# Bank adds ahead of VectorE's other work, row sums moved between the halves, and value chunks asked before the last unit

## The chip, the cores and the metric

The kernel runs on one core of a Trainium2 chip. The metric is the device time of one launch in microseconds (us). It has five engines with an instruction stream each: TensorE (PE, with its weight loads shown as PEld), VectorE (DVE), ScalarE (ACT), GpSimd (POOL) and SyncE (SP, which issues transfers). They are ordered only by semaphores that the program waits on.

## The reference

One layer of an encoder over 1024 tokens of width 1024 in float32: an RMS norm, a combined projection, a pooling mixer beside dilated window attention, an output projection, and then the expert layer (PEER), on which the change acts. Each token has 8 retrieval heads, each picks 16 of 16384 experts, and

```
ue = u[expert]
ve = v[expert]
act = gelu(einsum('thkd,td->thk', ue, ht))
return einsum('thk,thkd->td', gate * act, ve)
```

The layer's output is added to the residual stream and normed once more.

## The kernel before

The kernel has several stages; the first 1798 us (mixer, queries and their top 16, the products with all of `u`) are not touched. The change is in the last one, the products with `v`.

The 8 token tiles of 128 are treated in three ways. **Five tiles** (DT = 5) are computed densely: for each of 128 chunks of 128 experts, a matrix of weights (activation `a_raw` times gate `g_raw`, both reloaded from DRAM) is multiplied with the value chunk `v_raw`. **One tile** (PT = 1) gathers its value rows 4 x 128 at a time (`v_row`) and sums them by small matmuls into the two banks `wide`, 32 steps in all (`step`). **Two tiles** (VT = 2) gather their rows (`d_row`, a ring of 6) and VectorE adds each to `yg` with a weight (`add_row`, L1467): 256 row sums.

The dense part. Float32 accuracy comes from splitting: ScalarE rounds to `v_hi` and `a_hi`, VectorE computes the remainders `v_lo` (`lower_v`, L1474) and `a_lo` (`lower_a`, L1428), and TensorE does three products (L1881). The 128 chunks go in 16 groups of 8 (GT = 8). A group has two halves: first the 8 chunks with three tiles, then the same 8 chunks with two tiles, 32 halves in all. Every tile has two PSUM banks of 512 columns, so a half of three tiles fills banks 0 to 5 and one of two tiles banks 0 to 3. A product of three tiles is 18 matmuls of 128 x 128 by 512, one of two tiles is 12. At a half's end VectorE adds its banks to `y` in SBUF (`add_half`, L1440, two adds a tile); the first product of the next half waits, tile by tile, for the adds of the same banks (`y_done`).

VectorE's order is written out as a loop over n = 0 ... 255, one step per product. In step n it multiplies the weights of step n + 1 (`gated`, L1420), computes `a_lo` of step n, then if due the remainder of one value chunk of the next group (in the steps 13, 14, 15, 0, 1, 2, 3, 4 of each 16), a selection matrix (`pick`), row sums by `rows_added`, and, in steps 2 and 10 of 16, the adds of the half that has just ended. `rows_added(n)` spreads the 256 row sums evenly over the steps 3 to 238. `a_hi` and `a_lo` have 4 slots (RA = 4), so `a_hi` of step n waits for the product of step n - 4.

GpSimd issues the gathers: in its step n the rows of VectorE's step n + 2, moved on by the ring's 6, each after the row whose slot it takes was added; and after every `step` of TensorE four gathers of `v_row`.

SyncE's queue is in program order. The weights come in units of 4 chunks (`load_unit`: `a_raw` and `g_raw`, 0.75 MB each for three tiles, 0.5 MB each for two), four units a group; a unit waits until VectorE has multiplied all of the unit whose place it takes. The 8 value chunks of the next group (0.5 MB each, a ring of 6) are asked as 4 behind a group's second unit, 2 behind the third, 2 behind the fourth. The last two wait for the remainders of the next group's first two chunks.

At the start of the stage SyncE asks the five tiles of `y`, the two of `yg`, the value chunks 6 and 7, and then goes on with units.

Of the kernel before, what the change touches and what calls it, by code (L numbers as in the profile page):

```python
# [11 lines left out]
P = 128  # L12
# [24 lines left out]
DT = NT - NGT  # L37
DS = DT * P
MH = DS // 2
TT = (3, DT - 3)  # L40
# [23 lines left out]
GT = 8  # L64
NG = NK // GT
HALVES = 2 * NG
VJ = 4
# [2 lines left out]
PT = 1  # L70
VT = NGT - PT
DR = 6
STEPS = PT * P // 4
TILE_STEPS = P // 4
GROUP_STEPS = STEPS // NG
VR = 6
# [21 lines left out]
def steps_after(h, j):  # L98

    return [h] if j == {0: 6, HALVES - 1: 2}.get(h, 4) else []  # L100


def rows_added(n):

    return min(max((n - 3) * VT * P // (HALVES * GT - 20), 0), VT * P)


QT = S // 4
# [40 lines left out]
def build(nc, x, g_mix, w_in, w_pool, pool_scale, w_out, g_ffn, w_q, subkeys, u, u_rows, v, g_final,  # L149
          ident_c, iota_c, bias01_c, bias2_c, sel_c, edge_c, inv_c, out):  # L150
    ctx = ExitStack()
    with ctx:
        base = (nc.sbuf_base + 63) // 64 * 64

        def at(name, kb, shape, dt=F32):

            return nc.alloc_sbuf_tensor_at(name, shape, dt, offset=base + int(kb * 1024))

        def sem(name):
            return ctx.enter_context(nc.semaphore(name))  # L160
# [91 lines left out]
        y = [at(f"y{i}", base, [P, D]) for i, base in enumerate((64, 75, 112, 116, 120))]  # L252
# [20 lines left out]
        x1_d = nc.dram_tensor("x1_d", [NT, P, D], F32).ap()  # L273
# [74 lines left out]
        v_in = [sem(f"v_in{k}") for k in range(VR)]  # L348
        d_in = [sem(f"d_in{k}") for k in range(DR)]
        yd_in = sem("yd_in")  # L350
# [3 lines left out]
        y_in = sem("y_in")  # L354
# [58 lines left out]
        def half_width(h):  # L413

            return TT[h % 2] * P

        def tiles_done(h):

            return DT * (h // 2) + TT[0] * (h % 2)
# [16 lines left out]
        def _(sp):  # L436
# [83 lines left out]
            def load_v(j):  # L520

                if j >= VR:
                    sp.wait_ge(vl_done, j - VR + 1)
                sp.dma_start(v_raw[:, j % VR, :], v[j, :, :]).then_inc(v_in[j % VR], 16)

            def load_a(n):

                j, w, s = GT * (n // 4) + VJ * (n % 2), half_width(n // 2), n % 2
                t0 = n // 2 % 2 * WA
                sp.dma_start(a_raw[s][:, :, 0:w], act_d[j:j + VJ, :, t0:t0 + w]  # L530
                             .rearrange("j p t -> p j t")).then_inc(a_in[s], 16)

            def load_g(n):

                j, w, s = GT * (n // 4) + VJ * (n % 2), half_width(n // 2), n % 2
                t0 = n // 2 % 2 * WA
                sp.dma_start(g_raw[s][:, 0:w // TW, :], g_d[t0 // TW:(t0 + w) // TW, :, j:j + VJ, :]
                             .rearrange("b p j t -> p b (j t)")).then_inc(g_in[s], 16)

            def load_unit(n):  # L540

                sp.wait_ge(pd_done, VJ * (n - 1))
                load_a(n)
                load_g(n)
# [26 lines left out]
                sp.wait_ge(act_out[s], 16 * stores_before(ITEMS + s))  # L571
            sp.wait_ge(m1_done, 2 * ITEMS)
            sp.wait_ge(uh_gate, 1)
            for i in range(DT):
                sp.dma_start(y[i][:, :], x1_d[i]).then_inc(y_in, 16)
            sp.wait_ge(row_used, ROWS)
            for k in range(PT, NGT):
                sp.dma_start(yg[k][:, :], x1_d[DT + k]).then_inc(yd_in, 16)

            for j in range(VR, GT):  # L580
                load_v(j)
            for g in range(NG):
                more = range(GT * (g + 1), GT * (g + 2)) if g + 1 < NG else ()
                load_unit(4 * g + 2)
                load_unit(4 * g + 3)
                for j in more[:VJ]:
                    load_v(j)
                if more:
                    load_unit(4 * g + 4)
                for j in more[VJ:VR]:  # L590
                    load_v(j)
                if more:
                    load_unit(4 * g + 5)
                for j in more[VR:]:
                    load_v(j)
            sp.wait_ge(vl_done, NK)
            sp.dma_start(yg[0][:, :], x1_d[DT]).then_inc(ya_in, 16)
            sp.dma_start(gain2[:, :], bcast_row(g_final)).then_inc(gain_in, 16)
# [8 lines left out]
        def _(pool):  # L607
# [60 lines left out]
            def gather_v(k):  # L668

                n, s = k // 4, k % 4  # L670
                if n:
                    pool.wait_ge(step_done, n)
                else:
                    pool.wait_ge(ut_ev, 1)
                nc.gpsimd.indirect_dma_start(v_row[s][:, :], None, v_rows,  # L675
                                             bass.IndirectOffsetOnAxis(ids_t[:, 0, TW * s + n:TW * s + n + 1], 0)
                                             ).then_inc(row_in[s], 16)

            def gather_d(k):

                if k >= DR:
                    pool.wait_ge(yd_done, k - DR + 1)
                c = (PT + k % VT) * P + k // VT
                nc.gpsimd.indirect_dma_start(d_row[k % DR][:, :], None, v_rows,  # L684
                                             bass.IndirectOffsetOnAxis(ids[:, c:c + 1], 0)).then_inc(d_in[k % DR], 16)

            pool.wait_ge(row_used, ROWS)
            for k in range(2):
                pool.wait_ge(g_out[k], 16 * PAIRS)
            for k in range(DR):  # L690
                gather_d(k)
            for k in range(4):
                gather_v(k)
            for n in range(HALVES * GT):
                for k in range(*(min(rows_added(n + d) + DR, VT * P) for d in (2, 3))):
                    gather_d(k)
                for m in steps_after(n // GT, n % GT):
                    for s in range(4):
                        if m + 1 < STEPS:
                            gather_v(4 * (m + 1) + s)  # L700
# [326 lines left out]
        def _(dve):  # L1027
# [77 lines left out]
            for c in range(2):  # L1105
                for hf in range(2):
                    n = 2 * c + hf
# [54 lines left out]
            for n in range(GROUPS * UNITS + 2):  # L1162
# [6 lines left out]
                m = n - (GROUPS - 1) * UNITS - 6  # L1169
# [56 lines left out]
            for n, i in enumerate(ORDER):  # L1226
                dve.wait_ge(x_in[i], 32)
                for hf in range(2):
                    m = 2 * n + hf
# [194 lines left out]
            def lower_a(n):  # L1424

                dve.wait_ge(ah_done, n + 1)
                w = half_width(n // GT)
                V.tensor_tensor(a_lo[:, n % RA, 0:w], prod[:, n % 2, 0:w], a_hi[:, n % RA, 0:w],  # L1428
                                ALU.subtract).then_inc(al_done, 1)

            def add_half(h, q):

                n = tiles_done(h) + q
                dve.wait_ge(tile_done, n + 1)
                t = TT[0] * (h % 2) + q
                for c in range(2):
                    cols = slice(c * HALF, (c + 1) * HALF)
                    if h >= 2:
                        dve.wait_ge(y_done, 2 * (n - DT) + c + 1)
                    V.tensor_tensor(y[t][:, cols], y[t][:, cols], bank[2 * q + c][:, :], ALU.add).then_inc(y_done, 1)  # L1440
# [29 lines left out]
            def lower_v(g, j):  # L1470

                n = GT * g + j
                dve.wait_ge(vh_done, n + 1)
                V.tensor_tensor(v_lo[:, j, :], v_raw[:, n % VR, :], v_hi[:, j, :], ALU.subtract).then_inc(vl_done, 1)  # L1474

            gated(0)
            for n in range(HALVES * GT):
                if n + 1 < HALVES * GT:
                    gated(n + 1)
                if n < GT:  # L1480
                    lower_v(0, n)
                lower_a(n)
                done = n - RA - 1
                if done >= 0 and done // GT % 2 and done // GT + 1 < HALVES:
                    lower_v(done // GT // 2 + 1, done % GT)
                if n == 0:
                    dve.wait_ge(uh_act, 1)
                    V.tensor_tensor(uh[:, :].rearrange("p (t k) -> p t k", t=NGT),
                                    uh[:, :].rearrange("p (t k) -> p t k", t=NGT), gate_g[:, :, :],
                                    ALU.mult).then_inc(uh_gate, 1)  # L1490
                if n == 1:
                    dve.wait_ge(ut_done, 1)
                    V.tensor_copy(ids_t[:, :, :], wide[:, 0:PT * P].rearrange("p (t k) -> p t k", t=PT))
                    V.tensor_copy(gate_t[:, :, :], wide[:, HALF:HALF + PT * P]
                                  .rearrange("p (t k) -> p t k", t=PT)).then_inc(ut_ev, 1)
                    dve.wait_ge(ut_ev, 1)
                    for k in range(2):
                        pick(k)
                done = n - RA - 1
                if done >= 0:  # L1500
                    for k in steps_after(done // GT, done % GT):
                        if k % TILE_STEPS == TILE_STEPS - 1 and k + 1 < STEPS:
                            add_rows(k // TILE_STEPS)
                        if k + 2 < STEPS:
                            pick(k + 2)
                for k in range(rows_added(n), rows_added(n + 1)):
                    if k == 0:
                        dve.wait_ge(uh_gate, 1)
                        dve.wait_ge(yd_in, 16 * VT)
                    add_row(k)  # L1510
                h = n // GT
                if n % GT == 2 and h:
                    if h == 1:
                        dve.wait_ge(y_in, 16 * DT)
                    for q in range(TT[(h - 1) % 2]):
                        add_half(h - 1, q)
            add_rows(PT - 1)
            dve.wait_ge(gain_in, 48)
            for n, i in enumerate(FINAL):
# [503 lines left out]
```

## Time and profile before

| | us |
|---|---|
| median of 3 runs | 2845.58 (2843.27 to 2847.0) |
| profiled execution | 2851.25 |
| its span | 2849.5 |
| PE busy | 2694.0 (95%) |
| DVE busy | 2065.5 (72%) |
| POOL busy | 1415.5 (50%) |
| ACT busy | 904.6 (32%) |

The span is the time from the first to the last recorded instruction. The product stage starts near 1798 us. In the views a "waited for" line gives the total of the waits in us and their number; an idle time in square brackets stands behind the instruction that ended it, with what released it.

### The profile page before, as it was taken

What the parts mean: (1) busy time and instruction counts of PE and PEld (TensorE: products, weight loads), DVE (VectorE), ACT (ScalarE), POOL (GpSimd) and SP (SyncE); (2) the same over time, 40 slices, a digit from 0 to 9 for tenths busy, and PEclk for the clock granted to TensorE, in tenths of its full rate; (3) what the DMA queues carried; (4) which work ended last, traced back from release to release, by engine and by line L of the source; (5) the groups of instructions that cost most, each with busy time, mean ns of one, the idle gap of its engine ahead of it and who ended that gap; (6) DMA issues with size and microseconds to landing.
All of it is one profiled execution on the core that took longest, in us unless ns stands there. A gap on an engine that the chain in (4) does not pass through costs nothing.

```text
span 2849.5 us, 43062 instructions
## 1 busy us (share of the span) xinstructions
PE 2694.0 (95%) x15691; PEld 2359.4 (83%) x15691; DVE 2065.5 (72%) x4758; ACT 904.6 (32%) x1750; POOL 1415.5 (50%) x960
## 2 busy tenths in 40 slices
PE   7999979998999999999999999979999998999998
PEld 6776658998999999999999999757767776777776
DVE  6022263699888989999999953668787777778774
ACT  4222341322222222356666622312222222222222
POOL 1111030446566677765565565535565554656640
PEclk9999989999999999999999999989999999999999
DMA  3101031436777888899999999989999999999993
GB/s 140 45 30 30 23 121 51 126 116 224 247 273 258 285 280 275 281 334 381 382 377 377 384 342 332 340 308 358 349 369 359 330 365 326 352 368 358 354 331 135
DMA packets 301905, 763.34 MB, mean 268 GB/s; under 512 B 22992, under 2 KB 138064, under 8 KB 298960
## 3 DMA queue, kind: packets, MB, share of 16 engines
q0 software_dynamic: 110592, 402.70, 38.4%
q1 hardware_dynamic: 191184, 359.13, 36.6%
q8 instruction: 55, 0.90, 0.1%
q14 instruction: 74, 0.61, 0.1%
HBM read 669.47 MB, written 92.27 MB: 267 GB/s over the span
## 4 chain that ended last, share of the span: by engine, by line
PE 54%; DVE 19%; issue 7%; DMA 4%; POOL 2%; ACT 1%; another core or an unknown queue 0%; SPq 0%; DVEq 0%; ACTq 0%
PE bank L1537 22%; PE bank L1881 20%; PE bank L1845 5%; DVE u_row L1332 4%; DMA g_raw<-g_d 3%; PE bank L1773 2%; PE bank L1756 2%; DVE yg L1467 2%; DVE y L1440 1%; PE wide L1901 1%; POOL w_lo L622 1%; DVE prod L1420 1%; DVE rest_k L1259 1%; DVE ix L1262 1%; DVE eq L1319 1%
## 5 line engine op out<-in xcount | busy, mean ns | idle before, releaser
L1537 PE MATMUL bank<-h_hi,w_hi 128*128 128x320 f32 (+1 forms) x2400 | 574.4, 321 | 16.4 <-POOL w_lo L622 12.8
L1537 PE MATMUL bank<-h_hi,w_lo 128*128 128x320 f32 (+1 forms) x2400 | 557.5, 314 | 0.0
L1537 PE MATMUL bank<-h_lo,w_hi 128*128 128x320 f32 (+1 forms) x2400 | 557.1, 313 | 0.0
L622 POOL TENSOR_TENSOR w_lo<-w_raw,w_hi 128x1024 fp32r<-128x1024 f32 x144 | 368.2, 2557 | 336.1 <-ACT w_hi L910 280.7
L1332 DVE CUSTOM_DVE_ANT_0 u_row<-wide,u_row 128x1024 f32<-128x1024 f32 x384 | 450.3, 1221 | 80.1 <-DMA u_row<-in_u_rows,ids 73.2
L684 POOL DMA_INDIRECT d_row<-in_v,ids x256 | 368.2, 1438 | 277.3 <-DVE yg L1467 231.6
L1881 PE MATMUL bank<-v_hi,a_hi 128*128 128x512 f32 x1272 | 408.1, 403 | 73.2 <-DVE y L1440 59.9
L631 POOL DMA_INDIRECT u_row<-in_u_rows,ids x384 | 391.3, 1019 | 111.5 <-issue 76.8
L1537 PEld LDWEIGHTS bank<-h_hi,w_hi 128*128 128x128 f32 x2400 | 401.1, 190 | 22.9 <-POOL w_lo L622 14.6
L1537 PEld LDWEIGHTS bank<-h_lo,w_hi 128*128 128x128 f32 x2400 | 406.7, 189 | 3.9
L1537 PEld LDWEIGHTS bank<-h_hi,w_lo 128*128 128x128 f32 x2400 | 405.5, 189 | 3.9
L1881 PE MATMUL bank<-v_lo,a_hi 128*128 128x512 f32 x1272 | 401.1, 397 | 0.0
L1881 PE MATMUL bank<-v_hi,a_lo 128*128 128x512 f32 x1272 | 400.0, 396 | 0.0
L1881 PEld LDWEIGHTS bank<-v_hi,a_hi 128*128 128x128 f32 x1272 | 239.2, 192 | 158.6 <-DVE y L1440 69.0
L990 ACT ACTIVATE a_hi<-prod 128x384 fp32r<-128x384 f32 (+1 forms) x256 | 120.6, 471 | 741.1 <-PE bank L1881 605.8
L1467 DVE SCALAR_TENSOR_TENSOR yg<-d_row,uh,yg 128x1024 f32<-128x1024 f32 x256 | 326.3, 1281 | 6.4 <-issue 3.4
L1881 PEld LDWEIGHTS bank<-v_lo,a_hi 128*128 128x128 f32 x1272 | 244.1, 192 | 53.4
L1881 PEld LDWEIGHTS bank<-v_hi,a_lo 128*128 128x128 f32 x1272 | 244.3, 192 | 52.9
L611 POOL TENSOR_TENSOR w_lo<-w_raw,w_hi 128x1024 fp32r<-128x1024 f32 x36 | 87.0, 2418 | 404.8 <-ACT w_hi L707 404.8
L1428 DVE TENSOR_TENSOR a_lo<-prod,a_hi 128x384 fp32r<-128x384 f32 (+1 forms) x256 | 125.2, 489 | 222.9 <-ACT a_hi L990 185.6
L675 POOL DMA_INDIRECT v_row<-in_v,ids_t x128 | 181.2, 1416 | 194.2 <-PE wide L1901 133.4
L904 ACT ACTIVATE act_st<-bank 128x320 f32<-128x320 f32 x200 | 76.3, 432 | 338.7 <-PE bank L1537 238.4
(213 smaller groups left out, 3682.5 us busy)
## 6 DMA issues: line engine op xcount, KB each, us to landing
w_raw<-in_u SPq DMA_DIRECT2D x128, 512.0 KB
v_raw<-in_v SPq DMA_DIRECT2D x128, 512.0 KB
act_d<-act_st SPq DMA_DIRECT2D x128, 320.0 KB
g_d<-g_st SPq DMA_DIRECT2D x20, 2048.0 KB
a_raw<-act_d SPq DMA_DIRECT2D x32, 768.0 KB
g_raw<-g_d SPq DMA_DIRECT2D x32, 768.0 KB
w_raw<-in_w_q SPq DMA_DIRECT2D x32, 512.0 KB
a_raw<-act_d SPq DMA_DIRECT2D x32, 512.0 KB
```

Source lines behind the costliest of these rows:

```text
L611: nc.gpsimd.tensor_tensor(dst, w_raw[:, n % 2, :], hi, ALU.subtract).then_inc(lo_done, 1)
L622: nc.gpsimd.tensor_tensor(w_lo[:, s % 2, :], w_raw[:, s % 2, :], w_hi[:, s % 2, :], ALU.subtract).then_inc(lo_done, 1)
L631: nc.gpsimd.indirect_dma_start(u_row[k % RING][:, :], None, u_rows, bass.IndirectOffsetOnAxis(ids[:, k:k + 1], 0)).then_inc(row_in[k % RIN ...
L675: nc.gpsimd.indirect_dma_start(v_row[s][:, :], None, v_rows, bass.IndirectOffsetOnAxis(ids_t[:, 0, TW * s + n:TW * s + n + 1], 0)).then_in ...
L684: nc.gpsimd.indirect_dma_start(d_row[k % DR][:, :], None, v_rows, bass.IndirectOffsetOnAxis(ids[:, c:c + 1], 0)).then_inc(d_in[k % DR], 16)
L990: nc.scalar.activation(a_hi[:, n % RA, 0:w], prod[:, n % 2, 0:w], ACT.Copy).then_inc(ah_done, 1)
L1332: V.tensor_tensor_reduce(u_row[k % RING][:, :], wide[:, :], u_row[k % RING][:, :], 1.0, 0.0, ALU.mult, ALU.add, uh[:, k:k + 1]).then_inc(r ...
L1428: V.tensor_tensor(a_lo[:, n % RA, 0:w], prod[:, n % 2, 0:w], a_hi[:, n % RA, 0:w], ALU.subtract).then_inc(al_done, 1)
L1467: V.scalar_tensor_tensor(out=yg[t][:, :], in0=d_row[k % DR][:, :], scalar=uh[:, c:c + 1], in1=yg[t][:, :], op0=ALU.mult, op1=ALU.add).then ...
L1537: ins = pe.matmul(banks[h][:, 0:n], lhs[:, part], rhs[:, k, h * n:(h + 1) * n], start=(k == 0 and lhs is lhs_hi and rhs is h_hi), stop=(k ...
L1845: ins = pe.matmul(bank[4 + n % 2][:, k * NK:(k + 1) * NK], is_i[n % 4][:, k, :], gate_j[n % 4][:, k, :], start=True, stop=True)
L1881: ins = pe.matmul(bank[2 * q + c][:, :], lhs[:, j % RA, q * P:(q + 1) * P], rhs[:, j, c * HALF:(c + 1) * HALF], start=(j == 0 and rhs is v ...
```

## The change

Three edits. VectorE does the adds of a half (steps 2 and 10 of 16) right behind `a_lo`, ahead of the chunk's remainder, the selection matrix and the row sums. The row sums follow a table of 16 steps, `ROWS_PRODUCT`, with 17 in a period; they start in step 4 and end in step 244, and GpSimd's gathers follow the same function. SyncE asks the value chunks 4 to 7 of the next group between the third and the fourth unit, and the five loads of `y` behind the first unit of the stage instead of ahead of everything.

```diff
+ROWS_PRODUCT = (1, 0, 0, 0, 1, 2, 2, 2, 2, 2, 0, 2, 2, 0, 1, 0)
 def rows_added(n):
-    return min(max((n - 3) * VT * P // (HALVES * GT - 20), 0), VT * P)
+    full, m = divmod(n, 2 * GT)
+    return min(max(full * sum(ROWS_PRODUCT) + sum(ROWS_PRODUCT[:m]) - ROWS_PRODUCT[0], 0), VT * P)
...
             sp.wait_ge(uh_gate, 1)
-            for i in range(DT):
-                sp.dma_start(y[i][:, :], x1_d[i]).then_inc(y_in, 16)
             sp.wait_ge(row_used, ROWS)
...
                 load_unit(4 * g + 2)
+                if g == 0:
+                    for i in range(DT):
+                        sp.dma_start(y[i][:, :], x1_d[i]).then_inc(y_in, 16)
                 load_unit(4 * g + 3)
                 for j in more[:VJ]:
                     load_v(j)
                 if more:
                     load_unit(4 * g + 4)
-                for j in more[VJ:VR]:
+                for j in more[VJ:]:
                     load_v(j)
                 if more:
                     load_unit(4 * g + 5)
-                for j in more[VR:]:
-                    load_v(j)
...
                 lower_a(n)
+                h = n // GT
+                if n % GT == 2 and h:
+                    if h == 1:
+                        dve.wait_ge(y_in, 16 * DT)
+                    for q in range(TT[(h - 1) % 2]):
+                        add_half(h - 1, q)
                 done = n - RA - 1
                 if done >= 0 and done // GT % 2 and done // GT + 1 < HALVES:
                     lower_v(done // GT // 2 + 1, done % GT)
...
                     add_row(k)
-                h = n // GT
-                if n % GT == 2 and h:
-                    if h == 1:
-                        dve.wait_ge(y_in, 16 * DT)
-                    for q in range(TT[(h - 1) % 2]):
-                        add_half(h - 1, q)
```

## Rows read from the trace of the kernel before

**Rows 1.** The head of the page: the span, TensorE, and GB/s in 40 slices of 71 us

```profile
span 2849.5 us, 43062 instructions
PE 2694.0 (95%) x15691; PEld 2359.4 (83%) x15691; DVE 2065.5 (72%) x4758; ACT 904.6 (32%) x1750; POOL 1415.5 (50%) x960
GB/s 140 45 30 30 23 121 51 126 116 224 247 273 258 285 280 275 281 334 381 382 377 377 384 342 332 340 308 358 349 369 359 330 365 326 352 368 358 354 331 135
```

**Rows 2.** The adds of line L1440: who waited for them (us in all, times)

```profile
  PEld bank L1881: 69.0, 25
  PE bank L1881: 59.9, 19
```

**Rows 3.** Timeline of PE: start us, us, engine, line, names, count, [idle before, releaser]

```profile
2008.65 0.74 PE L1881 MATMUL bank<-v_hi,a_hi 128*128 128x512 f32 x2 [3.96 <-DVE y L1440]
2777.44 0.70 PE L1881 MATMUL bank<-v_hi,a_hi 128*128 128x512 f32 x2 [0.91 <-DVE y L1440]
```

**Rows 4.** Windows: length, PE, PEld, DVE, ACT, POOL busy, clock, DMA share, GB/s

```profile
2436.00:2452.00 16.00, 16.00 (x78) 11.81 (x78) 16.00 (x21) 7.24 (x12) 13.22 (x5) 1.00 0.97 328
2452.00:2468.00 16.00, 12.52 (x49) 9.90 (x48) 14.37 (x21) 4.58 (x7) 13.56 (x9) 0.89 1.01 366
```

**Rows 5.** Timelines of PE and DVE at the boundary of 2520 us

```profile
2520.25 0.61 PE L1881 MATMUL bank<-v_hi,a_lo 128*128 128x512 f32 x2
...
2519.85 0.56 DVE L1428 TENSOR_TENSOR a_lo<-prod,a_hi 128x384 fp32r<-128x384 f32 x1
2520.32 1.22 DVE L1474 TENSOR_TENSOR v_lo<-v_raw,v_hi 128x1024 fp32r<-128x1024 f32 x1
2521.45 1.28 DVE L1467 SCALAR_TENSOR_TENSOR yg<-d_row,uh,yg 128x1024 f32<-128x1024 f32 x1
2522.65 2.48 DVE L1440 TENSOR_TENSOR y<-y,bank 128x512 f32<-128x512 f32 x4
...
2523.99 0.74 PE L1881 MATMUL bank<-v_hi,a_hi 128*128 128x512 f32 x2 [3.12 <-DVE y L1440]
```

**Rows 6.** Lines of DVE, 2200 to 2700 us: count, busy us, mean ns, idle before

```profile
L1467 DVE SCALAR_TENSOR_TENSOR yg<-d_row,uh,yg 128x1024 f32<-128x1024 f32 x134 | 170.8, 1281 | 1.0 <-DMA d_row<-in_v,ids 1.0
L1474 DVE TENSOR_TENSOR v_lo<-v_raw,v_hi 128x1024 fp32r<-128x1024 f32 x60 | 73.2, 1220 | 0.0
L1428 DVE TENSOR_TENSOR a_lo<-prod,a_hi 128x384 fp32r<-128x384 f32 (+1 forms) x124 | 60.6, 489 | 106.5 <-ACT a_hi L990 88.6 <-issue 17.7
L1420 DVE TENSOR_TENSOR prod<-a_raw,g_raw 128x256 f32<-128x256 f32 (+1 forms) x124 | 60.2, 485 | 6.1 <-issue 6.1
L1440 DVE TENSOR_TENSOR y<-y,bank 128x512 f32<-128x512 f32 x79 | 48.9, 682 | 4.0 <-PE bank L1881 2.8 <-remote 1.2
```

**Rows 7.** Timeline of SP: last unit and last two value chunks of a group

```profile
2570.29 0.51 SPq L537 DMA_DIRECT2D g_raw<-g_d  x1
2570.84 4.20 SPq L524 DMA_DIRECT2D v_raw<-in_v  x2
```

**Rows 8.** Timeline of ACT: the longest wait for a value chunk

```profile
2400.20 1.06 ACT L982 ACTIVATE v_hi<-v_raw 128x1024 fp32r<-128x1024 f32 x1 [12.62 <-DMA v_raw<-in_v]
```

**Rows 9.** Timelines of SP, DVE and PE in the stage's first groups

```profile
1831.82 0.51 SPq L537 DMA_DIRECT2D g_raw<-g_d  x1
...
1863.47 0.56 DVE L1420 TENSOR_TENSOR prod<-a_raw,g_raw 128x384 f32<-128x384 f32 x1 [13.25 <-DMA g_raw<-g_d]
...
1864.41 1.22 PE L1881 MATMUL bank<-v_hi,a_hi 128*128 128x512 f32 x2 [7.99 <-DVE a_lo L1428]
...
1877.95 1.22 PE L1881 MATMUL bank<-v_hi,a_hi 128*128 128x512 f32 x2 [8.06 <-DVE y L1440]
```

**Rows 10.** Transfers of 2004 to 2776 us, and two windows as in rows 4

```profile
DMA packets 144623, 270.80 MB, mean 351 GB/s; under 512 B 7880, under 2 KB 93896, under 8 KB 144605
...
2020.00:2036.00 16.00, 16.00 (x79) 11.84 (x78) 7.74 (x11) 1.47 (x3) 4.16 (x5) 1.00 0.88 305
...
2100.00:2116.00 16.00, 15.34 (x67) 12.18 (x66) 13.78 (x22) 3.68 (x7) 7.47 (x8) 1.00 1.05 386
```

## The prediction

> **What bounds the kernel now.** I read the head of the page first: TensorE is busy 95% of the span [rows 1], so time can only come from the few stretches in which it stands, and a busy share of 95% hides half-speed work as well. Then I asked who waits for the bank adds, the line that the change moves: 19 matmuls waited 59.9 us for it, and their weight loads (the same stalls, seen on the other queue) 69.0 us [rows 2]. The product stage starts at 1798 us. TensorE's timeline through it shows these waits at the first product of a half. From 1950 us on, 13 stand before a half of three tiles and sum to 45.2 us, 3 before a half of two tiles (2.2 us); the three in the first groups are 8.06, 1.60 and 2.77 us. The first and the last of the 13 are in [rows 3], 12 groups apart: (2777.44 - 2008.65) / 12 = 64.07 us a group.
>
> After the longer stalls TensorE is slow as well. The stretch that holds such a start has a mean granted clock of 0.89, the one ahead of it 1.00 [rows 4]. Of the two levels, 2.4 and 1.2 GHz, a mean of 0.89 over 16 us is 22% at the lower one, 3.5 us, in which half the work is lost: 1.76 us at most; in the timeline it is four pairs of matmuls at 0.86 in place of 0.455 us, 1.6 us. It follows 9 of the 13, 14.4 us. Taken off the 12 periods: 768.8 - 43.5 (the waits after the first) - 14.4 - 1.2 (two short issue gaps) = 709.7, or 59.1 us of pure work a group. That is TensorE's floor.
>
> Why it waits is in one boundary [rows 5]. The last pair of the old half starts at 2520.25 and takes 0.455, so the half is done at 2520.7. VectorE starts `lower_a` of step 2 at 2519.85, then does a value chunk's remainder (0.47 after), a row sum (1.13 after), and only 1.20 later, at 2522.65, the adds. The next half starts at 2523.99. VectorE was also late at step 2: its `a_lo` needs the product one before the last, done 2.73 us (12 matmuls at 0.2275) before the half's end, and ScalarE's 0.5 us; it could have started about 2.0 us ahead of the end, and started 0.85 ahead.
>
> **The change part by part.**
> *The adds ahead.* What stood between is one remainder and one row sum: 1.13 + 1.20 = 2.33 us [rows 5]. Here the add could start at 2520.4 (the first tile's banks were complete 1.37 earlier). Two adds of a tile take 4 adds' 2.48 / 2 = 1.24, so the first tile is free near 2521.8 and the wait falls from 3.12 to about 1.0. Before three tiles only two had been used, and the second is free 1.24 later, while TensorE needs 1.37 for the first tile: it adds nothing. The added wait for the last tile holds VectorE about 1.3 us at this boundary and up to 3 us at the other. Behind it are chunk remainders and products of later steps, which have the four slots of `a_hi`/`a_lo` as cover (three products, 8.2 us at least). I cost it at nothing; without that cover it would be 3 us a group.
>
> *The row sums.* 17 per 16 steps instead of 17.36, at 1.20 each: 0.4 us of VectorE a group. What counts is where. From step 13 to step 1 of the next group, VectorE gives each product of 2.73 us two multiplies or subtracts, a remainder and a row: 0.34 + 0.34 + 1.13 + 1.20 = 3.0, so it falls behind. The new table has 2 rows there in place of 5.4, 4.1 us less. Steps 11 and 12 take 4 where they had 2.2, 2.2 us more, before. Step by step I get VectorE some 2 us late at step 13 and on time at step 1, with 0.5 to 1.3 us in hand. VectorE as a whole has the room: the five lines of 500 us sum to 414 us, with overlap in their records [rows 6]; from start to start a group is 16 products and 16 subtractions at 0.47 or, by their size, some 0.34 us (13.0), 8 remainders (9.0), 17 rows (20.4), 10 adds (6.2) and two picks (0.4), 49 us of 59.1. So the 1.0 us left above goes to between 0.1 and 1.0; I take 0.7, since a late row or chunk eats the margin. Then 13 waits of 3.48 become 0.7 (36 us), the three short ones go (2.2), and with stalls that short the clock stays up: the waits of 0.91 and 1.16 us have no slow pairs behind them (14.4 us).
>
> *Value chunks ahead of the last unit.* Chunks 6 and 7 of a group were asked behind its last unit (1.5 MB) [rows 7]; at 375 GB/s they land 4 us sooner. ScalarE's waits for them (up to 12.62 us [rows 8]) seldom end a TensorE stall. SyncE now passes two chunk waits (steps 13 and 14) before it asks the unit, so the unit is asked 1 to 5 us later; first used in step 3 of the next group, 19 us after its old ask, and by TensorE's fifth product. That is covered; I cost the swap at zero, between -1 us a group (a share of the clock-slowing stall at 2387) and +1.
>
> *Start.* The five loads of `y` go behind the first unit: 2.6 MB, 7 us, out of the way of `yg`, on which VectorE's first row waited 3.4 us, with no TensorE stall behind. In the first group step 16 waited 13.25 us for gates asked at 1831.82, landed at 1863.4; TensorE lost 7.99 and then 8.06 us [rows 9]. All bytes are still asked before that, and the table draws 11 rows by step 9 instead of 7, 2.1 MB or 5.6 us more in the queues. I take the first stall 3 us longer. The second falls: three rows and the order go, 8.06 to 3.5. With 1.60 and 2.77 and a slow stretch of 1.2 gone, the start gains 7 us (bounds 0 and 13).
>
> *The transfers.* They become the next limit. From 2004 to 2776 us they ran at 351 GB/s on average [rows 10], 22.57 MB in each of 12 parts. The 16 us windows that have a DMA share of 1.00 or more (25 of 54) average about 374 GB/s (386 in one), the one behind a boundary 305 at 0.88 [rows 10]; slices of the earlier row stage hold 377 to 384 [rows 1]. With 17 rows a group needs 22.4 MB: 59.9 us at 374, 58.3 at 384, 63.8 at 351. TensorE's floor with 0.7 is 59.8. Two limits that near each other do not overlap perfectly, and the row gathers are bunched (none in steps 1 to 3). I take 60.6 a group, between 59.3 and 63.8.
>
> The Trainium skill speaks against even that: "DMA: Bandwidth & Descriptors", Specifications, gives a core's limit to HBM as about 358 GB/s. By it a group would take an estimated 62.6 us. This trace exceeds it for 350 us on end (377 to 384 GB/s), so I do not go by it.
>
> **The sum.** 12 periods of 64.07 to 60.6: 41.6; the last boundary 0.5; the odd one before 2008 (3.96 and its slow stretch) 4; the start 7. Total 53 us. The profiled execution took 2851.25 us, 5.7 above the median; 2851.25 - 53 = 2798, and on the scale of the median 2793. The tail (final norms on VectorE) moves along unchanged.
>
> **Rivals.**
> *A. As forecast*, 2793, own range 2774 (59.3 a group, start 13) to 2812 (62 a group). Chance 0.62.
> *B. The transfers take most of it.* The stage ran at a DMA share near 0.98, SyncE already needs 4.20 us to issue two chunks where a unit's half goes out in 0.51 [rows 7], and row gathers are now bunched ahead of the fourth unit. If 355 GB/s is the mix's limit, a group takes 63.1: 12 us and 5 at the start, about 2828 (2812 to 2838). Against it: the windows at 374 to 386. The limit that the Trainium skill gives ("DMA: Bandwidth & Descriptors", Specifications) is this case too, at an estimated 62.6 a group and 2822. Chance 0.20.
> *C. Slower: the last-but-one unit comes late.* It is asked at step 10 and multiplied at step 15, some 17 us later. Steps 5 to 12 draw 3.5 rows more than before, 5 us of transfers, ahead of it or beside it. In the first group the same unit needed 31 us, and VectorE, held at step 15, reaches the adds late. The point: once the unit takes more than 18 us, each further us is a us of TensorE. At 24 us a boundary wait is 6 us with slow pairs, 7.6 against 4.8: 35 us more, about 2880; near 19 us it is no change. Against it: outside the first group and one at 2378 VectorE did not wait for units. Chance slower 0.10, and 0.05 for a draw within the noise.
> *D. The move does nothing*, since VectorE is late anyway and waits inside: the adds would start no sooner than `lower_a` at -0.85 us; that alone still takes 2.3 us off each boundary, so it is the upper end of A rather than a case; 0.03 for no change by it.
>
> **How the numbers follow.** The likeliest case gives 2793. 8 in 10: from 2772 to 2836, which takes in A and B. No change is within 0.2% (5.7 us), about what can be told here. Faster: A and B, 0.82; same 0.08 (the rest of C and D); slower 0.10.
>
> **What would show it.** Right: waits of TensorE for the bank adds fall from 59.9 to under 15 us, mean wait of a boundary under 1 us; the 16 us windows behind boundaries at clock 1.00; adds start within 0.6 us of `lower_a`'s start; a group 60 to 61 us; DMA about 370 GB/s. Wrong: ScalarE or VectorE waits of several us for units or rows in most groups (C), or groups of 63 us with DMA near 355 (B). First group: the 13 us wait still there.

## The result, and the profile after

| | before | after |
|---|---|---|
| median | 2845.11 us | 2876.99 us (2876.78 to 2877.64, 4 runs) |
| ratio | | 1.0112, 95% interval 1.0095 to 1.013 |
| profiled span | 2849.5 | 2875.0 |
| group of the product stage | 64.07 | 66.3 |

The change made the kernel 32 us slower, where 53 us less was forecast. The head of the page answers to [rows 1]: as many instructions, 9 us more of PE busy, and a lower mean rate of the transfers in the product stage (the numbers stand below).

```profile
span 2875.0 us, 43062 instructions
PE 2703.4 (94%) x15691; PEld 2367.7 (82%) x15691; DVE 2072.1 (72%) x4758; ACT 907.8 (32%) x1750; POOL 1350.3 (47%) x960
...
GB/s 139 44 30 30 23 132 57 113 132 219 251 262 282 275 276 278 291 344 382 376 377 376 378 332 319 366 318 339 339 320 325 343 344 347 344 345 347 344 337 143
```

Who waits for the bank adds, in the changed kernel (us in all, times; it answers to [rows 2], 69.0 and 59.9):

```profile
  PEld bank L1881: 79.8, 17
  PE bank L1881: 73.3, 17
```

So the very wait that the edit was to take away has grown. The first pairs behind two boundaries 11 groups apart, in PE's timeline, answer to [rows 3]: (2738.85 - 2009.49) / 11 = 66.3 us a group. Between them every half of three tiles starts behind a wait of 4.3 to 5.8 us, and slow pairs follow each time: mostly 1.22 us for the first pair, 0.73 at full clock. The granted clock behind one such start is 0.50, the level of 1.2 GHz (first line of the windows below).

```profile
2009.49 1.09 PE L1881 MATMUL bank<-v_hi,a_hi 128*128 128x512 f32 x2 [4.73 <-DVE y L1440]
...
2738.85 1.22 PE L1881 MATMUL bank<-v_hi,a_hi 128*128 128x512 f32 x2 [5.76 <-DVE y L1440]
```

One boundary, from the timelines of SP, DVE and PE (it answers to [rows 5] and [rows 7]):

```profile
2508.24 0.51 SPq L539 DMA_DIRECT2D g_raw<-g_d  x1
2508.79 12.08 SPq L526 DMA_DIRECT2D v_raw<-in_v  x1
...
2524.80 0.33 SPq L526 DMA_DIRECT2D v_raw<-in_v  x1
2525.17 0.52 SPq L532 DMA_DIRECT2D a_raw<-act_d  x1
...
2523.56 1.21 DVE L1474 TENSOR_TENSOR v_lo<-v_raw,v_hi 128x1024 fp32r<-128x1024 f32 x1
...
2530.08 0.56 DVE L1420 TENSOR_TENSOR prod<-a_raw,g_raw 128x384 f32<-128x384 f32 x1 [4.12 <-issue]
...
2533.85 0.62 PE L1881 MATMUL bank<-v_hi,a_lo 128*128 128x512 f32 x2
...
2538.04 0.55 DVE L1428 TENSOR_TENSOR a_lo<-prod,a_hi 128x384 fp32r<-128x384 f32 x1
2538.51 1.88 DVE L1440 TENSOR_TENSOR y<-y,bank 128x512 f32<-128x512 f32 x3
...
2539.85 1.22 PE L1881 MATMUL bank<-v_hi,a_hi 128*128 128x512 f32 x2 [5.38 <-DVE y L1440]
...
2548.04 0.56 DVE L1420 TENSOR_TENSOR prod<-a_raw,g_raw 128x384 f32<-128x384 f32 x1 [5.92 <-issue]
```

The adds do come 0.47 us behind the start of `a_lo`, as the edit says. But VectorE reaches step 2 only 3.7 us after the half's end (2538.04 against 2534.3), since it stood 4.12 us at step 15 for the third unit, asked at 2508.24 and used 21.8 us later. In all 12 groups of 2004 to 2776 us it is 21.4 to 22.6 us; in the kernel before the third unit was used 16.7 to 19.4 us after its ask without a wait, but for one group (20.3 us, a wait of 3.58). (The profile names no releaser, only "issue". The multiply of step 15 is the first of its unit: it waits for `a_in` and `g_in`, and for `a_hi` and `a_lo` of two steps before, which had been done, so it was the transfers.) Then at step 3 it stands 5.92 us for the last unit, asked at 2525.17, right behind the fourth chunk (2524.80); that chunk had waited for the slot which the remainder of step 14 frees (2523.56, 1.21 us). Between 2004 and 2776 us there are 23 such waits, 114.4 us, where the kernel before had 2, 6.1 us in all: 11 at step 15 (46.6 us) and 12 at step 3 (67.8 us). And some 8 us behind each boundary the transfers run dry. Windows of 4 us of the changed kernel behind the start at 2605.94 (columns as in [rows 4]):

```profile
2606.00:2610.00 4.00, 4.00 (x10) 3.13 (x11) 2.22 (x3) 0.29 (x1) 0.00 (x0) 0.50 1.05 384
2610.00:2614.00 4.00, 4.00 (x18) 3.31 (x17) 0.21 (x1) 0.00 (x0) 0.00 (x0) 0.95 1.13 322
2614.00:2618.00 4.00, 4.00 (x19) 3.31 (x18) 4.00 (x7) 1.05 (x2) 0.00 (x0) 1.00 0.58 151
2618.00:2622.00 4.00, 4.00 (x20) 3.30 (x19) 4.00 (x6) 0.53 (x1) 1.85 (x2) 1.00 0.13 17
2622.00:2626.00 4.00, 4.00 (x19) 3.34 (x18) 4.00 (x6) 0.53 (x1) 3.39 (x3) 1.00 0.76 225
2626.00:2630.00 4.00, 4.00 (x28) 2.30 (x27) 3.75 (x6) 0.42 (x1) 2.39 (x2) 1.00 1.10 374
2630.00:2634.00 4.00, 4.00 (x23) 2.91 (x16) 2.00 (x2) 0.00 (x0) 2.54 (x3) 1.00 1.03 409
```

The lowest in the same group of the kernel before, behind its stall:

```profile
2596.00:2600.00 4.00, 4.00 (x19) 3.32 (x18) 3.60 (x5) 0.53 (x1) 3.64 (x2) 1.00 0.88 299
2600.00:2604.00 4.00, 4.00 (x19) 3.31 (x18) 2.09 (x3) 0.53 (x1) 2.79 (x3) 1.00 0.87 284
```

After: 17 GB/s in one window and 391 to 411 in the seven from 2630. Set against 410, the three windows from 2614 lost 8.2 us of transfers, and little can make that up, for the other windows of this group average 390. Between 2004 and 2700 us, 21 windows of 4 us lie under 150 GB/s; before it was 3.

What is missing there are mostly the row gathers. SyncE's own pause behind the boundary is not new: it asks nothing from 2585.01 to 2599.63 before (14.6 us), and nothing from 2610.77 to 2623.05 after (12.3 us), when the multiply of step 6 frees the next unit's place. But GpSimd, which issues the gathers, is busy for 3.64 and 2.79 us in the two windows before and not at all from 2606 to 2618 after. Its first row gather in a group waits 14 us for a row sum (first line below; at most 10.4 us before). Part of that is the table, which has no row sum in steps 1 to 3: in the changed kernel with half rows (below), where no unit is late, the same wait is 6.4 to 7.9 us. Most of the rest is VectorE standing 5.6 us at step 3.

The rows suggest a circle: a late unit holds VectorE; a held VectorE frees no slot of units, chunks or rows; so little is asked and the engines idle; then everything is asked at once, and the unit in the middle of the burst is late. The mean of 2004 to 2776 us fell from 351 [rows 10] to 339 (second line). That transfers are the cause is shown below; how much each link of the circle carries is not.

```profile
2487.54 1.47 POOL L684 DMA_INDIRECT d_row<-in_v,ids  x1 [14.02 <-DVE yg L1467]
```

```profile
DMA packets 140405, 261.47 MB, mean 339 GB/s; under 512 B 7604, under 2 KB 91572, under 8 KB 140386
```

The first groups answer to [rows 9] (DVE, then PE; the kernel before has the last of these starts at 1944.10, behind 2.77 us):

```profile
1868.47 0.56 DVE L1420 TENSOR_TENSOR prod<-a_raw,g_raw 128x384 f32<-128x384 f32 x1 [13.44 <-issue]
...
1869.42 1.22 PE L1881 MATMUL bank<-v_hi,a_hi 128*128 128x512 f32 x2 [10.95 <-DVE a_lo L1428]
...
1878.23 1.22 PE L1881 MATMUL bank<-v_hi,a_hi 128*128 128x512 f32 x2 [4.08 <-DVE y L1440]
...
1943.30 0.73 PE L1881 MATMUL bank<-v_hi,a_hi 128*128 128x512 f32 x2 [3.75 <-DVE y L1440]
```

### The profile page after: what moved, and what is told of

It is laid out like the page before. It is cut to its first block, busy times and chain, and to the rows that moved or that the text cites. A ratio compares the mean times of both kernels' runs of the same rounds, so it can differ in the third digit from the quotient of the medians.

```text
span 2875.0 us, 43062 instructions
## 1 busy us (share of the span) xinstructions
PE 2703.4 (94%) x15691; PEld 2367.7 (82%) x15691; DVE 2072.1 (72%) x4758; ACT 907.8 (32%) x1750; POOL 1350.3 (47%) x960
## 4 chain that ended last, share of the span: by engine, by line
PE 56%; DMA 13%; DVE 9%; POOL 5%; issue 4%; ACT 1%; SPq 1%; DVEq 0%; ACTq 0%
PE bank L1537 28%; PE bank L1881 14%; DMA g_raw<-g_d 8%; PE bank L1845 5%; DMA d_row<-in_v,ids 5%; PE bank L1756 3%; PE bank L1773 2%; POOL v_row L675 2%; POOL d_row L684 1%; POOL w_lo L622 1%; PE wide L1901 1%; DVE u_row L1332 1%; DVE eq L1319 1%; DVE v_lo L1474 1%; PE bank L1782 1%
## 5 line engine op out<-in xcount | busy, mean ns | idle before, releaser
L684 POOL DMA_INDIRECT d_row<-in_v,ids x256 | 341.4, 1334 | 448.0 <-DVE yg L1467 404.3
L1420 DVE TENSOR_TENSOR prod<-a_raw,g_raw 128x384 f32<-128x384 f32 (+1 forms) x256 | 124.7, 488 | 180.2 <-issue 147.9
L675 POOL DMA_INDIRECT v_row<-in_v,ids_t x128 | 145.2, 1134 | 111.8 <-PE wide L1901 64.9
```

Of the source, the lines that this page charges most:

```text
L675: nc.gpsimd.indirect_dma_start(v_row[s][:, :], None, v_rows, bass.IndirectOffsetOnAxis(ids_t[:, 0, TW * s + n:TW * s + n + 1], 0)).then_in ...
L1420: V.tensor_tensor(prod[:, n % 2, 0:w].rearrange("p (b t) -> p b t", t=TW), a_raw[s][:, j, 0:w].rearrange("p (b t) -> p b t", t=TW), g_raw[ ...
```

## The experiments

Every kernel was timed in rounds beside the kernel before. Some kernels scatter (the adds alone from 2822 to 2850 us), so the ratios decide and not the profiled runs. The letters: A the early adds, R the table of row sums, C the last two chunks ahead of the last unit, Y the later loads of `y`. "Chunks early" and "half rows" are told below. Where a row has no R, the row sums are the even ones of the kernel before.

| kernel | median us | ratio to before, 95% |
|---|---|---|
| A | 2839.41 | 0.9973 (0.9952 to 0.9994) |
| R | 2847.57 | 1.0019 (1.0 to 1.0038) |
| C | 2854.94 | 1.0046 (1.0023 to 1.0069) |
| Y | 2847.91 | 1.0008 (0.9992 to 1.0025) |
| A R Y | 2867.43 | 1.009 (1.0065 to 1.0116) |
| A C Y | 2860.32 | 1.0054 (1.0032 to 1.0075) |
| R C Y | 2876.03 | 1.0105 (1.0068 to 1.0142) |
| A R C | 2872.22 | 1.0094 (1.0071 to 1.0116) |
| A R C Y (the change) | 2876.99 | 1.0112 (1.0095 to 1.013) |
| chunks early | 2838.72 | 0.9988 (0.9976 to 1.0001) |
| A R C Y, chunks early | 2816.01 | 0.9892 (0.9858 to 0.9927) |
| the same, table spread out | 2813.4 | 0.9884 (0.984 to 0.9928) |
| the same, table to the front | 2809.11 | 0.988 (0.9854 to 0.9906) |
| A R Y, chunks early | 2817.51 | 0.9909 (0.9876 to 0.9942) |
| A, chunks early | 2802.5 | 0.9863 (0.9834 to 0.9893) |
| A C, chunks early | 2800.02 | 0.983 (0.9792 to 0.9868) |
| before, half rows | 2815.85 | 0.9904 (0.987 to 0.9938) |
| A, half rows | 2777.29 | 0.9756 (0.972 to 0.9792) |
| A R C Y, half rows | 2760.39 | 0.9706 (0.9674 to 0.9737) |

**The edits one by one, and without the chunk order.** The diffs are the parts of the change's.

```diff
 A:  lower_a(n), then add_half(...), then lower_v, pick, add_row
 R:  rows_added(n) by ROWS_PRODUCT
 C:  for j in more[VJ:]: load_v(j)   ahead of   load_unit(4 * g + 5)
 A R Y: the change, with more[VJ:VR] ahead of the last unit and more[VR:] behind it
```

> Before with the first edit alone: a half's bank adds right behind a_lo. Theory R (the new table of row sums bunches the row gathers, and units and rows land late): without the table the adds start 2.3 us sooner, TensorE's 13 waits before a half of three tiles fall from 3.5 to 1.0 to 1.5 us and most slow pairs go; 30 to 45 us faster than before, about 2805 to 2815. Theory C (the unit asked behind the value chunks is the cause): the same here. Theory A (the early adds themselves hold VectorE, so that units are asked late): slower than before by 10 us or more, with VectorE waits for a unit at steps 15 and 3.

> Before with the table of row sums alone. Theory R: slower than before by 15 to 35 us, and VectorE waits for gathered rows (64 us between 2004 and 2776 us in the changed kernel, 1 us before) and 4 us for the unit of step 15 in each group. Theory C: no such waits, 10 to 25 us faster, since 4 us of row sums leave the stretch ahead of the boundary. Theory A: also faster.

> Before with the order of SyncE's asks alone: value chunks 6 and 7 ahead of the last unit (the loads of y stay where they were). Theory C: VectorE waits about 5.6 us for that unit in step 3 of each group, and the kernel is slower by 15 us or more. Theory R or A: that wait is small, since the step is not on TensorE's path; within 6 us of before.

> The changed kernel with the old order of value chunks and last unit (adds, table and the later loads of y stay). Theory R: still 2865 to 2880, row waits and the wait in step 15 stay, the 5.6 us wait in step 3 goes or moves. Theory C: the loss goes, 2790 to 2815. Theory A: 2865 to 2880 as well.

None of the three theories holds as stated. The adds alone win 0.27%, far less than 30 to 45 us: VectorE now waits for units there too (58.3 us, 18 times between 2004 and 2776 us, line below). The table alone costs 0.19% and C alone 0.46%, less than the 15 us written for each. The table alone does bring some of the signs of theory R, 20 waits for units (57.4 us) and 15 windows of 4 us under 150 GB/s between 2004 and 2700 us; the adds alone bring 12 such windows. So a dry stretch does not by itself make the loss. The loss comes from the edits together: A R Y loses 0.9%, against -0.27 + 0.19 + 0.08 = 0.0 for the sum of the three.

```profile
DVE prod L1420 <- issue: 58.3, 18, 8.1
```

**Which pair makes the loss.** Late adds with table and chunk order; early adds with chunk order and even row sums; `y` alone, and the change without it.

> The changed kernel with the old even row sums (early adds, chunk order and y's loads stay). If the table makes the burst: near the adds alone (2839) plus the chunk order's 10 us, 2840 to 2855, and the slowest 16th of a group no longer under 150 GB/s. If the early adds by themselves do: 2860 or more, as the changed kernel.

> The changed kernel with the adds in their old, late place. If the table alone is enough: 2865 or more. If it needs the early adds, which let VectorE fill all slots sooner: 2845 to 2860.

> The kernel before with the five loads of y behind the stage's first unit, and nothing else. If they matter only in the first group: within 6 us of before. If they set the phase in which all groups then run (a burst that is handed on): 10 us or more slower.

> The changed kernel with the loads of y in their old place. If they matter only in the first group: 2870 to 2880. If the move is a cause: 2860 or less.

R C Y loses 1.05% without the early adds, as much as the whole change (1.12%). A C Y loses 0.54%: at 2860 us it lies above the range written for the table as the cause (2840 to 2855), at the lower edge of the other. The expectation that the table needed the early adds was wrong. Its waits between 2004 and 2776 us, VectorE for units and PE for the adds, are about those of the changed kernel (114.4 and 62.4):

```profile
DVE prod L1421 <- issue: 114.7, 23, 6.1
...
PE bank L1882 <- DVE y L1441: 64.8, 12, 6.4
```

`y`'s loads have a small part at most: 1.0008 alone, and 5 us between the change with and without it, with intervals that overlap.

**Transfers or VectorE's order.** The row gathers fetch half of each row, and the row sum reads that half twice, so VectorE, GpSimd and TensorE have as many instructions in the same order.

```diff
-nc.gpsimd.indirect_dma_start(d_row[k % DR][:, :], None, v_rows, ...
+nc.gpsimd.indirect_dma_start(d_row[k % DR][:, 0:HALF], None, v_halves, ...
-  in0=d_row[k % DR][:, :]
+  in0=d_row[k % DR][:, 0:HALF].unsqueeze(1).broadcast_to([P, 2, HALF])
```

> The changed kernel whose row gathers fetch only half of each row (2 KB; the row sum reads that half twice, so the same number of elements is summed, but not the right ones). It takes 4.5 of 22.4 MB out of each group. Theory T: waits for units and rows vanish, waits before a half of three tiles fall under 1 us, and the group comes near its 59.1 us of matmuls: 2765 to 2790. Theory V: VectorE does the same work in the same order, so 2865 or more, at most 10 us faster than the changed kernel.

> The kernel before with the same halved row gathers (half of each row fetched, read twice). Theory T: before, TensorE's 3.5 us waits came from VectorE's order and not from transfers, so they stay; 2830 to 2846, and the changed kernel with halved gathers is faster than this one by 40 us or more: the sign of the edit turns with the transfers. Theory V: about the same here, but the changed one stays slower than this one.

> The kernel before with the early adds alone and halved row gathers (half of each row fetched and read twice). With transfers out of the way the prediction's step puts the adds at 2.3 us off each of 13 waits and all slow pairs, about 44 of the 55 us, the table at 0.3 to 0.9 us a wait: 2770 to 2780, waits of 1.0 to 1.7 us. If the table has the larger part: 2785 or more.

This is the run that decides. With 4.5 MB fewer a group the change is worth 2815.85 - 2760.39 = 55 us; the prediction's sum was 53. Both kernels came out faster than expected. The kernel before gained 30 us by half rows although most of its waits stayed; in the profiled runs 20.6 us of the gain lie in the first groups (the start of [rows 3] at 2008.65 stands at 1988.03). From one group to the next the changed kernel with half rows takes 59.0 us, about TensorE's floor of the prediction. Who waits for the adds: first the changed kernel with half rows (one wait left, in the first groups), then the kernel before with half rows.

```profile
  PEld bank L1884: 8.3, 14
...
  PE bank L1884: 2.2, 1
```

```profile
  PEld bank L1883: 51.7, 15
  PE bank L1883: 46.3, 16
```

The waits of the second are 2.8 to 4.0 us at each boundary but the last, much as in the full kernel before: those were VectorE's order and not transfers. With the adds alone it is 2777: 39 us are the adds', and 17 us are the table, the chunk order and `y`'s loads together, which were not parted. The waits left with the adds alone are 13.8 us at 11 boundaries, 1.25 each (1.0 was predicted):

```profile
PE bank L1883 <- DVE y L1441: 13.8, 11, 1.8
```

**Filling the gap in the asks.** Four value chunks are asked behind the first unit asked in a group, two behind the second. The kernel is the changed one otherwise. The second run also has a table with the 17 row sums spread out; it is not the even spread of the kernel before.

```diff
     load_unit(4 * g + 2)
+    for j in more[:VJ]:
+        load_v(j)
     load_unit(4 * g + 3)
-    for j in more[:VJ]:
+    for j in more[VJ:VR]:
         load_v(j)
     load_unit(4 * g + 4)
```

> The changed kernel with the value chunks asked where the DMA engines idle: four of the next group behind the group's second half's first unit (the first of the four asks) instead of behind the second, two behind the second instead of the third; the last two stay ahead of the last unit. Theory T (transfers: every buffer is full after a boundary, so nothing is asked for 9 us, and the burst behind it lands the unit of step 15 too late): 2 MB move out of the burst, worth 5 us at 400 GB/s; the 17 to 150 GB/s stretch fills, the waits for units fall from 4.1 to about 1 us, 30 to 60 us faster than the changed kernel, 2815 to 2845. Theory V (VectorE's own order, the early adds with the table, is the limit, and the idle transfers are a sign of it): within 8 us of 2870.

> As the previous one, and the table of row sums spread out: (1, 0, 0, 2, 1, 1, 2, 1, 1, 2, 0, 2, 1, 1, 1, 1), 17 in 16 steps as well. Theory T: the row gathers no longer come 12 in a row; another 10 to 25 us, 2790 to 2825, with row waits under 10 us in all (64 in the changed kernel). Theory V: four rows lie in steps 13 to 0 where the table had two, so VectorE reaches the adds later and it is slower than the previous one by 10 us or more.

61 us faster than the change, by the order of 6 asks. No window of 4 us between 2004 and 2700 us is under 150 GB/s, VectorE's waits for rows fall from 63.8 to 12.9 us, and PE's waits for the adds from 62.4 to 24.8. But theory T expected the waits for units to fall from 4.1 to about 1 us. In four of the 12 groups the third unit is used 16.0 to 17.0 us after its ask, with no stall of TensorE behind it; in the other eight it takes 20.6 to 21.2 us and VectorE still waits about 4 us at step 15. At step 3 the waits fell from 67.8 to 28.4 us. So the filled gap is shown to win the time; that it does so by landing the unit of step 15 sooner shows in a third of the groups. Spreading the table as well is worth nothing that can be told (0.9884 against 0.9892), where 10 to 25 us were expected.

```profile
DVE prod L1423 <- issue: 63.5, 20, 5.1
...
PE bank L1884 <- DVE y L1443: 24.8, 8, 4.6
```

> The kernel before (its adds, its even row sums, its last unit ahead of the last two chunks), only with four value chunks asked behind a group's first asked unit and two behind the second. Theory T (the gap of nothing asked behind a boundary, and the burst after it, is what the change made and what the earlier asks mend): before had no such gap (284 GB/s at its lowest), so little is won, 2830 to 2848. Rival U (the earlier asks are a gain of their own, 60 us wherever they are put, and the changed order of VectorE loses its 30 us as it did): 2780 to 2800 here.

> The early bank adds and the earlier asks of value chunks, with the old even row sums and the old place of the last unit. Theory T: the adds alone won 8 us with 58 us of waits for units; with the asks moved, 2800 to 2825, near the version that has the table as well (2816): the table gains nothing by itself. Rival (the table is what lets VectorE be on time): 2825 to 2840.

> Early adds, the table of row sums, the earlier asks, and the last two value chunks behind the last unit as before. If the last unit's place behind the chunks costs something (in the changed kernel VectorE waited 5.6 us for it in step 3 of each group), this is faster than the 2816 us of the version with the chunks ahead, by 5 to 20 us. If that wait was off the path, within 6 us of it, or slower by ScalarE's waits for the chunks.

> All three edits with the earlier asks, and a table whose row sums come sooner in a group: (1, 0, 0, 2, 2, 2, 2, 1, 1, 1, 0, 2, 2, 0, 1, 0). Theory T: three rows' slots come free 3 to 12 us sooner, where the engines still fell to 200 to 280 GB/s, and three gathers leave the burst: 5 to 20 us faster than 2816, and waits for units shorter than 3 us a group. Theory V (VectorE's own work is the limit): no gain or slower, since step 3 then has 4.5 us of work for a product of 4.1.

> The best version so far (early adds, even row sums, four chunks asked behind the first unit and two behind the second; 2802 us) with the last two chunks ahead of the last unit. If ScalarE's waits for these chunks (42 us there, up to 9 us) hold TensorE: 5 to 15 us faster. If the last unit's later landing costs as much: within 5 us. If it costs more, as in the kernel before (10 us): 2808 to 2820.

The early asks alone win nothing clear (0.9988): the kernel before had hardly a gap to fill (3 windows under 150 GB/s), so they are a remedy and no gain of their own. With the early adds and the *old, even* row sums they give 2802.5, and 2800.0 with C: the two differ by 0.3% with intervals that overlap. The versions with the table are 15 to 16 us slower (2816.0 and 2817.5 with it, 2800.0 and 2802.5 without), the spread-out one 13, the one with its rows to the front 9. These pairs differ in `y`'s loads too, and their intervals touch, so the table's price here is likely and not shown. In the 2802 us kernel VectorE waits 6.2 us for units in all, the third unit is used 17.2 to 20.1 us after its ask, the waits at the boundaries are 0.5 to 3.6 us, and no window of 4 us from 2004 to 2700 us is under 200 GB/s (258 in the group shown). A group is (2603.32 - 1931.35) / 11 = 61.1 us. Its waits of 2004 to 2776 us, two starts in PE's timeline 11 groups apart, and that window:

```profile
PE bank L1881 <- DVE y L1440: 20.5, 11, 3.6
...
DVE prod L1420 <- issue: 6.2, 3, 2.9
```

```profile
1931.35 0.73 PE L1881 MATMUL bank<-v_hi,a_hi 128*128 128x512 f32 x2 [1.64 <-DVE y L1440]
...
2603.32 0.73 PE L1881 MATMUL bank<-v_hi,a_hi 128*128 128x512 f32 x2 [1.70 <-DVE y L1440]
```

```profile
2540.00:2544.00 4.00, 2.30 (x11) 1.58 (x10) 4.00 (x8) 2.49 (x3) 3.09 (x4) 1.00 0.81 258
```

## Why the prediction was wrong

*What bounds it, and the adds: right.* The 13 waits are VectorE's order. The step "the wait falls from 3.12 to about 1.0" holds at 1.25 with half rows, and at 0.5 to 1.8 in all but two groups of the 2802 us kernel, with no slow pairs behind them. In the full changed kernel it was 4.3 to 5.8, since the adds came 0.47 us behind `a_lo` as said but `a_lo` of step 2 itself came 3.7 us behind the half's end.

*The row sums: right for VectorE at most, wrong for the kernel.* With half rows the table, the chunk order and `y`'s loads together take away the last 1.25 us and 17 us of time; the table's own part was not measured. The step looked at the table as VectorE's load alone. It is the timetable of GpSimd's gathers as well.

*Start: the stalls right, the gain not.* First stall 3 us longer: 7.99 became 10.95. Second 8.06 to 3.5: it is 4.08. But the stall of 2.77 us, which was to go, became 3.75, and there the changed kernel is 0.8 us ahead (1943.30 against 1944.10) where 7 were forecast.

*"I cost the swap at zero."* Its term was mis-sized: C alone costs 0.46%, 13 us (0.23 to 0.69%), and inside the change the last unit took 22.9 us from ask to use (2525.17 to 2548.04) where 19 were thought ample. It was asked 14.7 us ahead of the next half's start, 17.0 before, the delay of 1 to 5 us that was foreseen. The wait of 5.9 us lies in step 3, off TensorE's path as said, but it holds VectorE when VectorE should free slots, and that was not counted.

*The transfers: the step that failed.* "I take 60.6 a group, between 59.3 and 63.8" divided the group's bytes by the mean rate of busy windows. The rate was even too low (windows of 400 to 411 GB/s after, 374 taken): bytes alone would have allowed 22.4 / 0.41 = 54.6 us. A group took 66.3. What it left out is that a transfer is asked only when VectorE has freed its place, so that when it is asked and landed counts and not the sum of the bytes: the third unit took 21.8 us from ask to use where 16.7 to 19.4 had been enough, and TensorE waited 4.3 to 5.8 us at each boundary where 0.7 was forecast. A schedule that takes 14 of its 17 rows in steps 5 to 12 and 2 in the seven after leaves the engines dry behind a boundary (15 windows under 150 GB/s by the table alone, 21 in the change). The limit of some 358 GB/s that the Trainium skill gives ("DMA: Bandwidth & Descriptors", Specifications) was not what bound it either: seven windows in a row lie above 390.

*Rival C named it*, place and price: the unit asked at step 10 and multiplied at step 15, past 18 us each us counts, "at 24 us ... about 2880". It took 21.8 us, and the time is 2877. That the times meet is in part luck: by C's own rule 21.8 us makes a boundary wait of 3.8, with slow pairs 5.4 against 4.8, 7 us in all, about 2853. The measured waits are longer since the adds start 4.2 us behind the half's end. It had a chance of 0.10, since "outside the first group and one at 2378 VectorE did not wait for units". That evidence was of the old timetable of gathers, which is what the change replaced. Its size was miscounted too: the table has 14 rows in steps 5 to 12, the even spread 8.7, so 5.3 more and not 3.5. Yet C had one cause, rows ahead of the unit; the dry stretch behind the boundary is part of it too, for filling it wins back 61 us with the row gathers as bunched as before.

What stays open: why C costs 13 us by itself (its profiled run was as fast as that of before, with 7 waits for units of 12.4 us in all), and how the edits share the loss. R C Y loses 1.05% without the early adds and A R Y 0.9% without C, but A C Y without the table only 0.54%: the table with either of the other two is enough for most of it, and why they add up to more than their sum is not shown.

## What to carry to other kernels

Moving work within an engine's queue also moves every transfer whose buffer that work frees. When the transfers run at 98% of the time, as here, draw up when each is asked and landed, not how many bytes there are: a mean rate says nothing of when one unit lands. And before a table or an order is judged, run it once with halved transfers: here that showed that the edit is worth 55 us where the transfers do not stand in its way.

## What had not been expected of the hardware

The same transfers ran at 391 to 411 GB/s in seven windows of 4 us in a row, and at 403 to 406 in several slices of 19 us of the changed kernel. The kernel before reaches 410 in single windows of 4 us, but only one of its 16 us windows (400) passed 391. SyncE's issue of one 0.5 MB chunk can take 12.08 us (at 2508.79; in the kernel before one took 15.86, at 2373.46), where that of the fourth chunk of the same group takes 0.33. The chunk behind the long one is asked only at 2520.91. The last unit is not late by it, since it follows the fourth chunk, which waited for its slot until 2524.77.
